# Expert token rows sent through a DRAM table and transposed, in place of selection products, with the expert loops written out

## The reference

```
def swiglu(x, w1, w3, w2):
    return (jax.nn.silu(x @ w1) * (x @ w3)) @ w2

def moe(hn, w_router, w1, w3, w2):          # hn: 256 x 1024, w1, w3: 8 x 1024 x 2816, w2: 8 x 2816 x 1024
    top_v, top_i = lax.top_k(t @ w_router, 2)
    top_w = jax.nn.softmax(top_v, axis=-1)
    ...
    for e in range(8):
        out = out + combine[:, e:e + 1] * swiglu(t, w1[e], w3[e], w2[e])
```

## Time and profile before

| | |
|---|---|
| median of 3 runs | 1356.41 us (1354.2 to 1357.6) |
| the profiled execution | 1354.73 us, of which the span (first to last instruction) is 1350.5 us |
| mean granted TensorE clock | 0.993 of full speed |
| PE busy | 1312.4 us (97%), 6066 matmuls |
| DVE, ACT, POOL busy | 1061.7 us (79%), 877.3 us (65%), 65.6 us (5%) |
| moved by DMA | 382.12 MB, mean 283 GB/s |
| the experts | from 571.0 us, first matmul of expert 0, to 1340.7 us |

### The profile page before, as it was taken

The page is one execution under the profiler, slowest core; times in us unless marked ns, Lnnn a source line. Parts: engine busy times, 40 slices in busy tenths (PEclk is TensorE's granted clock), DMA queues, the critical chain, the costliest instruction groups (busy, mean ns, idle before and its releaser), DMA issues.

```text
span 1350.5 us, 17653 instructions
## 1 busy us (share of the span) xinstructions
PE 1312.4 (97%) x6066; PEld 1076.6 (80%) x6066; DVE 1061.7 (79%) x983; ACT 877.3 (65%) x870; POOL 65.6 (5%) x45
## 2 busy tenths in 40 slices
PE   7899999999999999799999999999999999999998
PEld 6688888888888788678888778788888788788776
DVE  5857756665457667699898799898898897998996
ACT  6567444444365664577777677777777777777774
POOL 0500000000006010000000000000000000000200
PEclk9999999999999999899999999999999999999999
DMA  9654546555555544289998899998999997999993
GB/s 360 242 190 133 167 146 221 184 187 187 192 183 175 168 150 163 94 302 369 388 384 324 316 410 372 377 374 293 389 405 380 368 357 281 411 386 385 410 355 141
DMA packets 105488, 382.12 MB, mean 283 GB/s; under 512 B 11952, under 2 KB 11952, under 8 KB 105392
## 3 DMA queue, kind: packets, MB, share of 16 engines
q1 hardware_dynamic: 103632, 375.11, 76.2%
q0 software_dynamic: 1616, 5.77, 1.1%
q10 hardware_dynamic: 144, 0.01, 0.0%
HBM read 376.12 MB, written 4.72 MB: 282 GB/s over the span
## 4 chain that ended last, share of the span: by engine, by line
PE 83%; DVE 6%; DMA 5%; ACT 2%; issue 2%; POOL 1%; SPq 1%; POOLq 0%; DVEq 0%; ACTq 0%
PE ps L391 26%; PE ps L393 25%; PE ps L392 25%; DMA raw<-in_units 4%; DVE wl L386 3%; PE ps L881 3%; ACT wh L378 1%; PE ps L1175 1%; DMA cols<-y_rows,yidx 1%; DMA y_rows<-xs 1%; POOL rst L514 1%; PE ps L933 0%; SPq L371 0%; DVE turn_t L1350 0%; POOL back L562 0%
## 5 line engine op out<-in xcount | busy, mean ns | idle before, releaser
L386 DVE TENSOR_TENSOR wl<-raw,wh 128x2048 fp32r<-128x2048 f32 x351 | 802.3, 2295 | 179.2 <-ACT wh L378 170.8
L378 ACT ACTIVATE wh<-raw 128x2048 fp32r<-128x2048 f32 x351 | 673.7, 1920 | 227.0 <-PE ps L393 206.3
L391 PE MATMUL ps<-wh,XT_h 128*128 128x512 f32 x1228 | 491.3, 400 | 15.4 <-DVE wl L386 12.7
L393 PE MATMUL ps<-wh,XT_l 128*128 128x512 f32 x1228 | 480.4, 391 | 0.0
L392 PE MATMUL ps<-wl,XT_h 128*128 128x512 f32 x1228 | 479.3, 390 | 0.0
L391 PEld LDWEIGHTS ps<-wh,XT_h 128*128 128x128 f32 x1228 | 231.1, 188 | 68.0 <-DVE wl L386 12.5
L393 PEld LDWEIGHTS ps<-wh,XT_l 128*128 128x128 f32 x1228 | 231.0, 188 | 50.3
L392 PEld LDWEIGHTS ps<-wl,XT_h 128*128 128x128 f32 x1228 | 231.5, 189 | 44.9
L391 PE MATMUL ps<-wh,moe_gT_h 128*128 128x512 f32 x352 | 138.0, 392 | 0.0
L393 PE MATMUL ps<-wh,moe_gT_l 128*128 128x512 f32 x352 | 137.1, 390 | 0.0
L392 PE MATMUL ps<-wl,moe_gT_h 128*128 128x512 f32 x352 | 137.0, 389 | 0.0
(11 more groups left out here) (235 smaller groups left out, 909.9 us busy)
## 6 DMA issues: line engine op xcount, KB each, us to landing
raw<-in_units SPq DMA_DIRECT2D x704, 512.0 KB, 5.9
y_rows<-xs POOLq DMA_DIRECT2D x7, 512.0 KB, 7.4
mix<-in_xT SPq DMA_DIRECT2D x2, 512.0 KB, 5.6
raw<-in_units SPq DMA_DIRECT2D x4, 256.0 KB, 8.4
h<-in_x SPq DMA_DIRECT2D x1, 1024.0 KB, 12.1
out<-h SPq DMA_DIRECT2D x2, 512.0 KB, 3.0
rows<-in_rows SPq DMA_DIRECT2D x1, 896.0 KB, 15.1
cols<-in_cols SPq DMA_DIRECT2D x1, 512.0 KB, 14.5
```

The lines of the kernel that those rows point to most:

```text
L378: nc.scalar.activation(wh[:, U.split_slot(j), :], raw[:, U.raw_slot(j), :], ACT.Copy).then_inc(hi_ready, 1)
L386: nc.vector.tensor_tensor(wl[:, s, :], raw[:, U.raw_slot(j), :], wh[:, s, :].bitcast(F32), ALU.subtract).then_inc(lo_ready, 1)
L391: nc.tensor.matmul(o, xh, bh, start=start, stop=False)
L393: return nc.tensor.matmul(o, xl, bh, start=False, stop=stop)
```

## The change

Token rows of experts 2 to 7 no longer come from selection products:

1. **Zeros.** In layer 0 POOL issues eight DMAs of 512 KB, DRAM to DRAM, that fill rows 0 to 1023 of a new table `x_rows` with zeros.
2. **Rows out.** In slice 1 of expert 0, after its sigmoid, ACT scales both token tiles into `back0` and `back1` (`token_rows`, 2 ACTIVATEs of 128 x 1024). `row_indices` makes one more set of indices (2 more small DVE operations); POOL then issues four indirect writes of 128 rows x 4 KB (`send_rows`).
3. **Rows in.** POOL loads two experts' rows with two DMAs of 512 KB into `back2` and `back3` (`load_rows`): for (2, 3) in expert 0, for (4, 5) and (6, 7) after the transposes of the pair before.
4. **Transposes.** In the down half of experts 1, 3, 5, PE transposes them (`rows_T`): 8 transposes of 128 x 128 ahead of u = 0, 8 ahead of u = 2, each four into one bank. ACT and DVE split each bank (`rows_hi`, `rows_lo`) at u = 1 and u = 3, ahead of the split of the unit that stands there.
5. **Selection matrices** for the pairs are no longer made in slices 8 and 9 of experts 1, 3 and 5; expert 7's own is made in its slice 2.
6. **Loops.** All expert loops on SP, PE, ACT, DVE and POOL are written out in Python.

```diff
+            def send_rows():
+                pool.wait_ge(yidx_ready, 1)
+                pool.wait_ge(hn_rows, 1)
+                pool.wait_ge(x_zero, 16 * E)
+                for t in range(TT):
+                    for a in range(2):
+                        pool.indirect_dma_start(x_d[:, :], bass.IndirectOffsetOnAxis(ap=xidx[:, a, t:t + 1], axis=0),
+                                                back[t][:, 0:D], None).then_inc(x_sent, 16)
+            def load_rows(k):
+                if k == 1:
+                    pool.wait_ge(x_sent, 64)
+                else:
+                    pool.wait_ge(xr_tr, 4 * (k - 1))
+                for b in range(2):
+                    pool.dma_start(back[2 + b][:, 0:D], x_d[(2 * k + b) * P:(2 * k + b + 1) * P, :]).then_inc(x_back, 16)
-            store_rows(0, 0)
-            with pool.Fori(0, E // 2 - 1) as i:
-                store_rows(2 * i + 1, 1)
-                store_rows(2 * i + 2, 0)
+            send_rows()
+            load_rows(1)
+            for p in range(E - 1):
+                if p in (1, 3):
+                    load_rows((p + 3) // 2)
+                store_rows(p, p % 2)
...
+            def token_rows():
+                act.wait_ge(y_sent, 16)
+                for t in range(TT):
+                    ins = nc.scalar.activation(back[t][:, 0:D], xs3[:, t, :], ACT.Copy, scale=rn[:, t:t + 1])
+                ins.then_inc(hn_rows, 1)
+            def rows_hi(k, r):
+                act.wait_ge(xr_tr, 4 * (k - 1) + r + 1)
+                nc.scalar.activation(XT_h[:, 2 * r:2 * r + 2, :], ps[:, 6 + r % 2, :].rearrange("p (c n) -> p c n", c=2),
+                                     ACT.Copy).then_inc(xr_hi, 1)
...
+            def rows_T(k, r):
+                if r == 0:
+                    pe.wait_ge(x_back, 32 * k)
+                if r >= 2:
+                    pe.wait_ge(xr_lo, 4 * (k - 1) + r - 1)
+                for a in range(2):
+                    for b in range(2):
+                        c = 2 * r + a
+                        last = transpose(ps[:, 6 + r % 2, a * SEQ + b * P:a * SEQ + (b + 1) * P],
+                                         back[2 + b][:, c * P:(c + 1) * P])
+                last.then_inc(xr_tr, 1)
                 for u in range(SLICES):
-                    if u < 2 and gather_next:
-                        gather(*gather_next, u)
+                    if u in (0, 2) and next_rows is not None:
+                        rows_T(next_rows, u)
+                        rows_T(next_rows, u + 1)
...
+            def rows_lo(k, r):
+                dve.wait_ge(xr_hi, 4 * (k - 1) + r + 1)
+                v = ps[:, 6 + r % 2, :].rearrange("p (c n) -> p c n", c=2)
+                tt(XT_l[:, 2 * r:2 * r + 2, :], v, XT_h[:, 2 * r:2 * r + 2, :].bitcast(F32), ALU.subtract)\
+                    .then_inc(xr_lo, 1)
...
-            expert(0, 0, Units(MOE_BASE), 0, 0, rank, FFN_UNITS + 1, None)
-            with dve.Fori(0, E // 2 - 1) as i:
-                U = Units(MOE_BASE + FFN_UNITS, i, 2 * FFN_UNITS)
-                expert(2 * i + 1, 1, U, 0, 2 * i + 1, rank, FFN_UNITS + 1, 2 * i + 2)
-                expert(2 * i + 2, 0, U, FFN_UNITS, 2 * i + 2, rank, FFN_UNITS + 1, None)
+            for p in range(E - 1):
+                expert(p, p % 2, U, p * FFN_UNITS, p, rank, FFN_UNITS + 1, (p + 1) // 2 if p % 2 else None)
```

More of the change, by code:

```diff
@@ L480, in _ @@
                         load_unit(sp, U, u, DENSE_BASE + u)
[L481 to L486, removed]
+            U = Units(MOE_BASE)
+            for j in range(E * FFN_UNITS):
+                load_unit(sp, U, j, MOE_BASE + j)
             sp.wait_ge(table_ready, 1)
@@ L540, in _ @@
                 root(rn[:, :], ssq[:, 0:TT])
+                if l == 0:
+                    for e in range(E):
+                        pool.dma_start(x_d[e * P:(e + 1) * P, :], zeros_d).then_inc(x_zero, 16)
             pool.wait_ge(unit_used, MIX_BASE[1] + MIX_UNITS)
@@ L824, in hi, with expert @@
                     .then_inc(g_hi, 1)
-            def expert(p, b, U, j0, last_split, gather_next, first=None, scatter=None):
+            def expert(p, b, U, j0, last_split, next_rows, first=None, scatter=None):
                 if first is not None:
@@ L837, in expert @@
                         hi(p + 1, j - 2)
+                    if j == 1 and isinstance(p, int) and p == 0:
+                        token_rows()
                     if j == 7 and scatter is not None:
@@ L1205, in scatter, with expert @@
                                  xs3[:, b, n * 512:(n + 1) * 512], start=True, stop=True).then_inc(sc_done, 1)
-            def expert(p, b, U, j0, first, x_ready, gather_next, scatter_at=None):
+            def expert(p, b, U, j0, first, x_ready, next_rows, scatter_at=None):
                 if first:
@@ L1243, in _ @@
             last.then_inc(counted, 1)
[L1244 to L1249, removed]
+            U = Units(MOE_BASE)
+            for p in range(E - 1):
+                expert(p, p % 2, U, p * FFN_UNITS, None, (xr_lo, 4 * (p // 2)) if p >= 2 else (gat_cp, 8),
+                       (p + 1) // 2 if p % 2 else None)
+            expert(E - 1, 1, U, (E - 1) * FFN_UNITS, None, (xr_lo, 12), None, 0)
             pe.wait_ge(table_ready, 1)
@@ L1731, in add_back, with expert @@
                 stt(v, ps[:, 6 + r % 2, :], comb[:, t, bass.ds(e, 1)], v, ALU.mult, ALU.add).then_inc(h_add, 1)
[L1733 removed]
+            def expert(p, b, U, j0, e, places, last_split, next_rows, scatter_at=None, first=False):
                 if first:
@@ L1746, in expert @@
                         row_indices()
[L1747 to L1750, removed]
+                    if j == 2 and isinstance(p, int) and p == E - 1:
+                        dve.wait_ge(gat, 8)
+                        select(b, e, places)
                     for a in range(2):
@@ L1758, in expert @@
                         lo(p, SLICES - 1)
+                    if u in (1, 3) and next_rows is not None:
+                        rows_lo(next_rows, u - 1)
+                        rows_lo(next_rows, u)
                     if 2 * SLICES + u + AHEAD <= last_split:
@@ L1856 @@
     tensors = [("x", inp["x"]), ("xT", xT), ("positions", np.ascontiguousarray(inp["positions"].reshape(TT, P).T))]
-    tensors += [("units", unit_order(inp)), ("cols", cols), ("rows", rows)]
+    tensors += [("units", unit_order(inp)), ("zeros", np.zeros((P, D), np.float32)), ("cols", cols), ("rows", rows)]
     for name, a in tensors:
```

57 lines of the change are left out of this document (36 added, 21 removed).

## The result

The kernel after takes **1338.35 us** (median of 4, 1336.58 to 1338.9) against 1355.31 us before (4 runs in the same comparison): ratio 0.988, 95% interval [0.9855, 0.9905]. The forecast was 1345.2 with a range from 1341.0 to 1350.5. The direction was right and so was the way in which each of the two large terms works; the size was too small, and the range missed the time by 2.65 us. In the profiled executions it is 1338.71 against 1354.73 us, 16.0 less where the sum said 11.2.

A forecast was written before the change was run, and what follows sets the result against it. PE, with 83% of the chain of waits, was taken to bound the kernel. Terms -14.1 + 6.3 - 7.4 + 2.7 + 1.0 + 0.3 = -11.2 us gave 1345.2 us against the median, range 1341.0 to 1350.5.

The forecast's parts named there:

- gathers out: Experts 1, 3, 5: removing the three gathers of token rows by selection products saves 4.7 us each, -14.1 us.
- transposes in: Down halves of experts 1, 3, 5: PE's transposes 5.0 us plus late splits 1.3 us, +6.3 us together.
- loop edges, within the span: Experts 1, 2, 3, 5, 6: writing out the loops removes the stalls at their edges, -7.4 us; bounds 0 to 7.4.
- expert 0: Expert 0: copies and small operations ahead of splits +2.7 us; DMAs taking queue time from the weights +1.0 us.
- expert 7: Expert 7, slice 2: two selects ahead of `add_rows`, partly covered by DVE's wait for rows, +0.3 us; bounds 0 and 0.6.
- The late units: Expert 0: the new row DMAs put the weights behind, +1.0 us; bounds 0 and 15.4.
- The split of the edges between engines: Loop edges: SP's pauses cost PE 0.9, 1.7 and 1.0 us; experts 3 and 5 lose 1.6 and 2.2 us.
- B: Rival, loop edges: instruction-fetch stalls stay in the longer program, so -7.4 falls away; 1352.6 us, chance 0.08.
- C: Rival, down halves of experts 1, 3, 5: DVE becomes the bound, 13.2 us instead of 6.3; 1352.1 us, chance 0.05.
- D: Rival, mainly expert 0: row DMAs make weights late, 15.4 us in place of 1.0; 1359.6 us, chance 0.07.

The follow-up runs named there:

- loops_out: The kernel before with all expert loops (SP, PE, ACT, DVE, POOL) written out, selection products kept; 1345.18 us, ratio 0.9933.
- no_send: The kernel after without the four indirect writes of token rows; expert 0 takes 96.45 us in place of 97.57.
- sp_out: The kernel before with only SP's loop written out; 1354.01 us.
- pe_loop: The kernel before with every expert loop written out but PE's; 1355.64 us.
- dve_act_loop: The kernel before with only the loops of DVE and ACT kept, the others written out; 1345.19 us.
- lo_twice: The kernel after with each of the twelve subtractions that split the transposed rows done twice; experts 1, 3 and 5 take 95.7 us, 1.17 more.
- sp_loop: The kernel after with only SP's loop put back; 1339.01 us.
- rows_early: The kernel after with ACT's two scaled copies and DVE's row indices moved to before expert 0; 1331.86 us.

## Why the prediction was wrong in size

By the steps of its sum, in us, against the profiled executions:

| step | forecast | measured | from |
|---|---|---|---|
| gathers out | -14.1 | -14.2 | 3 x (97.50 - 92.77), `loops_out` |
| transposes in | +6.3 | +5.3 | 3 x (94.53 - 92.75), after |
| loop edges, within the span | -7.4 | -7.3 | 578.11 - 570.80, `loops_out` |
| loop edges, outside the span | not seen | -2.2 | 4.23 to 2.01 |
| expert 0 | +3.7 | +3.4 | 97.57 - 94.20 |
| expert 7 | +0.3 | -0.8 | 96.59 - 97.37 |
| ahead of expert 0, behind expert 7 | 0 | -0.1 | 571.04 to 570.65, and 9.78 to 10.07 |
| sum | -11.2 | -15.9 | the times themselves: -16.0 |

**The step that failed first is the term "Loop edges out: -7.4".** It was read inside the span only, where it measured 7.3; with the time outside the span the loops were worth 9.5. The front table had 1354.73 us beside a span of 1350.5; I used the 4.2 us between them as a constant. They are 3.6 to 4.3 us in the kernels that keep PE's loop and 1.8 to 2.2 us in those that don't; what happens in them no row shows. My bounds for the term, 0 to 7.4, had no room for it.

**"Transposes in" was mis-sized by 1.0.** PE in the down half of expert 1 of the kernel after:

```profile
730.54 0.27 PE L928 MATMUL ps<-cols,back 128*128 128x128 f32 x1
730.65 0.27 PE L928 MATMUL ps<-cols 128*128 128x128 f32 x1
...
731.33 0.48 PE L403 MATMUL ps<-wh,moe_gT_h 128*128 128x512 f32 x1
...
737.16 0.27 PE L928 MATMUL ps<-cols,back 128*128 128x128 f32 x1
...
737.95 0.48 PE L403 MATMUL ps<-wh,moe_gT_h 128*128 128x512 f32 x1
```

From the first of eight transposes to the next matmul it is 0.79 us, and no wait of PE shows in the rest of the expert. By the end marks a pair costs 1.78 us (94.53 - 92.75): the 1.66 of the earlier trace rows and 0.12. The 0.45 us a pair that I added for late splits is 0. DVE still had 0.84 us idle between its subtractions and the pair of splits for units 25 and 26:

```profile
735.67 1.28 DVE L1783 TENSOR_TENSOR XT_l<-ps,XT_h 128x512 fp32r<-128x512 f32 x2
737.80 4.49 DVE L398 TENSOR_TENSOR wl<-raw,wh 128x2048 fp32r<-128x2048 f32 x2 [0.84 <-ACT wh L390]
742.21 1.28 DVE L1783 TENSOR_TENSOR XT_l<-ps,XT_h 128x512 fp32r<-128x512 f32 x2
```

The Trainium skill (TensorE: Matmul & The Clock Gate, Part 4: PE-mode transpose) gives about 275 ns for a bf16 transpose in one kernel's context. The fp32 ones here agree with that as a length, 0.27 us a record, but the next one starts 0.11 us later, and the pace is what counts in a run.

**"Expert 7: +0.3" had the wrong sign.** The four indirect loads were issued faster. POOL in the kernel after, and DVE beside the third load:

```profile
1239.53 1.39 POOL L595 DMA_INDIRECT back<-y_rows,yidx  x1 [8.07 <-DMA y_rows<-xs]
1241.22 2.12 POOL L595 DMA_INDIRECT back<-y_rows,yidx  x1 [0.30 <-issue]
1243.54 0.47 DVE L1686 TENSOR_SCALAR sel_r<-cols,rank 128x128 fp32r<-128x128 f32 x2
1243.65 0.98 POOL L595 DMA_INDIRECT back<-y_rows,yidx  x1 [0.31 <-issue]
1244.94 2.09 POOL L595 DMA_INDIRECT cols<-y_rows,yidx  x1 [0.30 <-issue]
```

The third load in the kernel before, and DVE beside it:

```profile
1256.86 2.28 DVE L386 TENSOR_TENSOR wl<-raw,wh 128x2048 fp32r<-128x2048 f32 x1
1256.96 2.99 POOL L562 DMA_INDIRECT back<-y_rows,yidx  x1 [0.31 <-issue]
```

The third takes 0.98 us where it took about 3.0 in the five kernels with the old gathers, and the rows are there sooner: DVE waits 0.17 us in place of 0.99. The new row writes are not the reason, since `no_send` has 0.97 us too. What DVE does beside it fits. Before, the third load starts 0.1 us into a split that ends at 1259.14, and its issue ends 0.81 us after that. After, the first of the two selects stands in that place, ends at 1243.82, and the issue ends 0.81 us after that. It is so throughout: of the 80 indirect issues in the thirteen traces, 72 start while DVE works, and 71 of them end 0.80 to 0.92 us after that DVE instruction; the 8 that find DVE idle take 0.95 to 1.05 us. So the two selects, which I had priced as a cost ahead of `add_rows`, most likely let the third load through. No run moved them alone.

**Expert 0 was right, and by its steps.** ACT's two copies take 2.18 us at 577.27 us and the first pair of splits starts at 581.28, 1.7 us later by the clock of the trace and 2.1 from expert 0's start, where I had said 2.3. The indices, put at 0.4, cost the 0.2 that is left. The late units cost 1.12 us (`no_send`), where I had said 1.0. Some luck is in the last digit, since the other kernels with the same expert 0 give up to 0.4 us more.

**The split of the edges between engines held for the kernel before and is no price list.** I put 3.6 us on SP's pauses and 3.8 on PE's jumps, and `sp_out` gave the 3.6 back in experts 1, 2 and 6. But there PE's two edges rose from 3.8 to 8.4 us, and the whole gained nothing. With SP's code straight, all of the cost hangs on PE's loop (`pe_loop`, `dve_act_loop`). Edges don't add.

The rivals: B did not come about (no pause at any former edge). C is refuted by the 1.78 us a pair and by `lo_twice`. D came in small, at 1.1 us; why no more than that was not tried. By the figure of about 358 GB/s that the Trainium skill (SBUF — State Buffer, A bandwidth-pool intuition that's wrong (but worth ruling out)) gives, the change would have been a little slower than before, as estimated in the prediction. The windows at 410 to 416 GB/s above disagree with that figure, and the change was faster.

The last 2 us of the miss are none of the sum: the profiled execution before was 1.7 us below its median, the one after 0.4 above, and I carried the first over.

## What to carry to other kernels

Read a repeating stage by marks that repeat: the clean repetition gives the pace, and each one's surplus is a cost with a place. A hardware loop on a TensorE that never idles can cost microseconds at every jump back (1.6 to 4.3 here), the more so if the clock falls behind the pause, and some more outside the span; write it out first and see, it is the cheapest of changes. Price an edge by what it costs next to the others as they are: one engine's edge grew when another's was taken away. When a rival wins, look whether it won for its reason: the pauses of `sp_loop` were nearly as long as before, and only their cost was gone. Look for the holes ahead of and behind a full stage before putting new work into it: the same copies, indices and additions, with the late units that they bring, cost some 8 us inside it and almost nothing outside.

## What I had not expected of the hardware

- Six pauses of PE of 2.08 to 2.55 us, four at its jump back (`sp_out`, `pe_loop`) and two in expert 7 (`loops_out`, `dve_act_loop`), are each followed by some 3 us at half clock (matmuls 0.43 us apart in place of 0.23). The twelve of 0.94 to 1.93 us in the expert stage of these four kernels, of the one before and of the one after are not.
- SP's pause at its jump back is 5.5 to 7.7 us, and differs as much between the rounds of one loop as between kernels.
- Between 1.8 and 4.3 us of an execution lie outside its span, and they follow PE's loop.
- An indirect DMA's issue on POOL takes 0.95 to 1.05 us with DVE idle; beside a running DVE instruction it ends 0.80 to 0.92 us after that one's end, so it took up to 3.0 us.
- Four indirect row writes of 0.5 MB each took 9.7 us with the queues nearly idle (`rows_early`), 4.8 of it the issuing, and from 588.84 to 607.78 us, 18.9, beside the weights, 10.4 of it the issuing behind DVE's splits.
